# Paired steps of four gated networks: where the first weight sum is formed, and which buffer holds the second one's low part

## The chip, the cores and the metric

The kernel runs on one core of a Trainium2 chip. The metric is the device time of one execution in microseconds (us), as the median of several runs. TensorE multiplies matrices, VectorE (DVE), ScalarE (ACT) and GpSimd (POOL) work element by element, SyncE (SP) issues the loads. Each engine takes its own instructions in order, and they are tied together by semaphores.

## What is computed

A model of two blocks over 256 tokens of 1024 numbers each: several mixers, a routed mixture of experts, and four gated networks. The change touches the gated networks alone:

```python
def swiglu(x, w_gate, w_up, w_down):
    return (jax.nn.silu(x @ w_gate) * (x @ w_up)) @ w_down

f = swiglu(rms_norm_2(x, g[4]), ffn_w_gate[layer, 1], ffn_w_up[layer, 1], ffn_w_down[layer, 1])
x = x + 0.5 * rms_norm_2(f, g[5])
```

The hidden width is 2816. All weights are 32-bit.

## The kernel before

**Steps.** Each network (`ffn0` to `ffn3`) runs in 11 steps of 256 hidden columns. A step has three units of weights of 128x2048 numbers, 1 MB each: two for gate and up (the upper and the lower half of the 1024 inputs), one for down. A unit is loaded into a ring of five buffers (`ring`, `load`, L815 ff.), and then split for precision: ScalarE writes its high part (L994), VectorE its low part (L1718), both into one of four slots (`w_a`, `w_b`). TensorE multiplies high by high, high by low and low by high, three matmuls in place of one.

**Pairs.** Steps 3 and 4 are done together, and so are 7 and 8 (`PAIRS`). Tokens are halved, inputs are halved, and the two steps' columns are the halves of the output: a 2x2 by 2x2 product of blocks, done by the Winograd form of Strassen's scheme with seven products instead of eight. It needs four sums of the tokens' blocks (once a network) and four of the weights' blocks. With the units named b11 and b21 (step s) and b12 and b22 (step s+1), VectorE forms:

- t1 = b12 - b11, into the buffer `w_sum`
- t3 = b22 - b12, over b12 in the ring
- t2 = t3 + b11, over b11 in the ring
- t4 = b21 - t2, over b21 in the ring

t2, t4 and t1 are split too. Their high part goes, one after the other, into one buffer, `sum_hi` (ScalarE: L1401, L1411, L1416). The low part of t2 and t4 goes to `ring_lo`, a second buffer beside each buffer of the ring, that of t1 to `w_sum_lo` (VectorE, all by `sum_left`, L2385). t3 is split like any unit.

**TensorE's order in a pair** (`pair`, from L3487 on, `product` at L3479 with the lines L3483 to L3485, 12 matmuls each): the product of b11; the transpositions of step s-1 (L3440); m6 with t2; the product of b21; m7 with t3; half of step s-1's down product (L3449 to L3451); m4 with t4; the other half; the product of b22; the transpositions of step s; m5 with t1; step s's down product. The step before a pair is an ordinary one: gate and up (L3424 to L3426) in two halves, transpositions, down.

**VectorE's order around a pair** is written out by hand, in `gated` and `pair` (L2398 ff.). In step s-1: a product (`hid_made`, L2336), a low part of the turned one (`hid_left`, L2343), `weight_sums` (t1 at L2371, t3 at L2373), the split of b21, `hid_made`, `more_weight_sums` (t2 at L2378, t4 at L2380), t2's low part, two splits. Before the first pair of a network it also has `x_left` (L2392). In the pair: `hid_left`, c_12 (`joined`, L2395, after m6), the split of b22, `hid_made`, t4's low part, c_22 (after m7), the split of the next unit, c_21 (after m4), t1's low part, `hid_made`, and so on. ScalarE's order (`pair_ahead`, `pair`) mirrors it.

**The ring.** A buffer is loaded anew once its unit is split. The two buffers that hold t2 and t4 are freed by others (`RELEASE`): b11's by the end of m6 and b21's by the end of m4. The loads are in one queue, so each waits for those before it; the unit that goes to b11's buffer is the down unit of step s, the first that the pair still needs.

Of the kernel before, what the change touches and what calls it, by code (L numbers as in the profile page):

```python
# [9 lines left out]
ALU = mybir.AluOpType  # L10
# [13 lines left out]
RING = 5  # L24
# [246 lines left out]
def build(nc, x, gains, stream, small_1, cmp_w1, small_2, consts, slots, out):  # L271
# [3 lines left out]
    with ExitStack() as ctx:  # L275
# [14 lines left out]
        ring = sb("ring", [P, RING, UNIT])  # L290
# [377 lines left out]
        m_1, c_12, c_22, c_21 = (sm1[:, 512 * n:512 * n + 512] for n in range(4))  # L668

        FFNS = ["ffn0", "ffn1", "ffn2", "ffn3"]  # L670
        PAIR_DVE = ["t1", "t3", "t2", "t4", "t2_lo", "u2", "t4_lo", "u3", "c21", "t1_lo", "w", "c12", "c22"]
        FFN_DVE = ["x_raw", "s1", "s2", "s3", "s4", "s_lo"] + [f"{step}_{i}" for i in range(len(PAIRS)) for step in PAIR_DVE]
        FFN_ACT = ["s_hi"] + [f"{step}_{i}" for i in range(len(PAIRS)) for step in ("t2_hi", "m1", "t4_hi", "t1_hi")]
        FFN_PE = [f"{step}_{i}" for i in range(len(PAIRS)) for step in ("m6", "m7", "m4", "m5")]
# [1 line left out]
        def ffn_at(steps, name, step):  # L676

            return SPARSE_STEPS + FFNS.index(name) * len(steps) + steps.index(step) + 1
# [61 lines left out]
        for name in FFNS:  # L740
            for i, s in enumerate(PAIRS):
                b11, b21, _, _ = pair_units(name, s)
                RELEASE[b11] = ("ffn_pe", ffn_at(FFN_PE, name, f"m6_{i}"))
                RELEASE[b21] = ("ffn_pe", ffn_at(FFN_PE, name, f"m4_{i}"))

        def tops_done(name, s):
# [210 lines left out]
        def _(act):  # L957
# [414 lines left out]
            def gated(name):  # L1372
# [30 lines left out]
                def pair(i, s):  # L1403
                    b11, b21, _, _ = pair_units(name, s)
                    act.wait_ge(S("unit_used"), b11 + 1)
                    act.activation(m_1, bank[4][:, :], ACT.Copy).then_inc(S("ffn_act"), 1)
                    hid_in(s - 1, range(0, 2))
                    split_at(3 * s + 3)
                    act.wait_ge(S("ffn_dve"), ffn_at(FFN_DVE, name, f"t4_{i}"))
                    act.wait_ge(S("ffn_pe"), ffn_at(FFN_PE, name, f"m6_{i}"))  # L1410
                    act.activation(sum_hi[:, :], ring[:, b21 % RING, :], ACT.Copy).then_inc(S("ffn_act"), 1)  # L1411
                    act.wait_ge(S("unit_used"), b21 + 1)
                    silu_of(bank[4], 0)
                    split_at(3 * s + 4)
                    act.wait_ge(S("ffn_pe"), ffn_at(FFN_PE, name, f"m4_{i}"))
                    act.activation(sum_hi[:, :], w_sum, ACT.Copy).then_inc(S("ffn_act"), 1)  # L1416
                    act.wait_ge(S("ffn_dve"), ffn_at(FFN_DVE, name, f"c21_{i}"))
                    silu_of(c_21, 1)
                    split_at(3 * s + 5)
                    hid_in(s, range(0, 2))  # L1420
                    split_at(3 * s + 6)
                    for t, c in enumerate((c_12, c_22)):
                        act.wait_ge(S("ffn_dve"), ffn_at(FFN_DVE, name, f"c{t + 1}2_{i}"))
                        silu_of(c, t)
                    split_at(3 * s + 7)
                    split_at(3 * s + 8)
# [278 lines left out]
        def _(dve):  # L1705
# [619 lines left out]
            def gated(name):  # L2325
# [35 lines left out]
                    own("s2")  # L2361
                    dve.tensor_tensor(x_sum[:, 3], a12, x_sum[:, 1], ALU.subtract).then_inc(S("ffn_dve"), 1)

                def weight_sums(i, s):
                    b11, b21, b12, b22 = pair_units(name, s)
                    raw = [ring[:, b % RING, :] for b in (b11, b21, b12, b22)]
                    if i:
                        dve.wait_ge(S("ffn_pe"), ffn_at(FFN_PE, name, f"m5_{i - 1}"))
                    dve.wait_ge(S(f"unit{b11 % RING}"), 16 * (b11 // RING + 1))
                    dve.wait_ge(S(f"unit{b12 % RING}"), 16 * (b12 // RING + 1))  # L2370
                    dve.tensor_tensor(w_sum, raw[2], raw[0], ALU.subtract).then_inc(S("ffn_dve"), 1)  # L2371
                    dve.wait_ge(S(f"unit{b22 % RING}"), 16 * (b22 // RING + 1))
                    dve.tensor_tensor(raw[2], raw[3], raw[2], ALU.subtract).then_inc(S("ffn_dve"), 1)  # L2373

                def more_weight_sums(i, s):
                    b11, b21, b12, _ = pair_units(name, s)
                    own(f"t3_{i}")
                    dve.tensor_tensor(ring[:, b11 % RING, :], ring[:, b12 % RING, :], ring[:, b11 % RING, :], ALU.add).then_inc(S("ffn_dve"), 1)  # L2378
                    own(f"t2_{i}")
                    dve.tensor_tensor(ring[:, b21 % RING, :], ring[:, b21 % RING, :], ring[:, b11 % RING, :], ALU.subtract)\  # L2380
                       .then_inc(S("ffn_dve"), 1)
# [15 lines left out]
                def pair(i, s):  # L2397
                    b11, b21, _, b22 = pair_units(name, s)  # L2398
                    hid_left(s - 1, range(0, 2))
                    dve.wait_ge(S("ffn_act"), ffn_at(FFN_ACT, name, f"m1_{i}"))  # L2400
                    dve.wait_ge(S("ffn_pe"), ffn_at(FFN_PE, name, f"m6_{i}"))
                    joined(c_12, bank[7], m_1)
                    split_at(3 * s + 3)
                    hid_made(s, 0)
                    ring_left(f"t4_hi_{i}", b21)
                    dve.wait_ge(S("ffn_pe"), ffn_at(FFN_PE, name, f"m7_{i}"))
                    joined(c_22, bank[7], m_1)
                    split_at(3 * s + 4)
                    dve.wait_ge(S("ffn_pe"), ffn_at(FFN_PE, name, f"m4_{i}"))
                    joined(c_21, bank[7], m_1)  # L2410
                    sum_left(f"t1_hi_{i}", w_sum_lo, w_sum)
                    hid_made(s, 1, c_21)
                    dve.wait_ge(S("unit_used"), b22 + 1)
                    own(f"u2_{i}")
                    joined(c_12, bank[4], c_12)
                    hid_left(s, range(0, 2))
                    split_at(3 * s + 5)
                    dve.wait_ge(S("ffn_pe"), ffn_at(FFN_PE, name, f"m5_{i}"))
                    own(f"w_{i}")
                    joined(c_12, bank[5], c_12)  # L2420
                    joined(c_22, bank[5], c_22)
                    hid_made(s + 1, 0, c_12)
                    split_at(3 * s + 6)
                    hid_made(s + 1, 1, c_22)
                    split_at(3 * s + 7)
                    split_at(3 * s + 8)
# [6 lines left out]
                for s in range(1, last):  # L2433
# [7 lines left out]
                    if s + 2 == PAIRS[0]:  # L2441
                        x_whole()
                    if ahead is not None:
                        weight_sums(ahead, s + 1)
                    split_at(3 * s + 3)
                    hid_made(s, 1)
                    if ahead is not None:
                        more_weight_sums(ahead, s + 1)
                        ring_left(f"t2_hi_{ahead}", pair_units(name, s + 1)[0])
                    split_at(3 * s + 4)  # L2450
                    if s + 2 == PAIRS[0]:
                        x_sums()
# [397 lines left out]
        def _(pe):  # L2850
# [533 lines left out]
            def gated(name, then):  # L3384
# [103 lines left out]
                def pair(i, s):  # L3488
# [7 lines left out]
                    product(4, own[0], whole[0], True).then_inc(S("unit_used"), 1)  # L3496
                    turn(s - 1, range(0, 2))
                    sum_ready(f"t2_lo_{i}")
                    product(7, both[1], (sum_hi[:, :], ring_lo[:, b11 % RING, :]), True).then_inc(S("ffn_pe"), 1)
                    pe.wait_ge(S("ffn_act"), ffn_at(FFN_ACT, name, f"m1_{i}"))  # L3500
                    lo_ready(b21)
                    product(4, own[1], whole[1], False).then_inc(S("unit_used"), 1)
# [541 lines left out]
```

## Time and profile before

| | |
|---|---|
| runs, us | 1793.16, 1794.06, 1794.82 (median 1794.06) |
| profiled execution, us | 1793.34 |
| its span, us | 1790.4 |
| TensorE busy, us | 1754.3 (98%) |
| VectorE busy, us | 1389.7 (78%) |
| ScalarE busy, us | 995.0 (56%) |
| t1, L2371 | 8 times, 2280 ns in the median |

The profile is of one execution. The span runs from its first to its last instruction on the core; the execution's time is 2.9 us longer. A busy time is a sum over the whole span and doesn't say which wait ends last at a place, so the timelines of single stretches are needed. In them a row has a start, a duration and the engine, then line, operation and tensors. Brackets tell how long the engine was idle before and what released it. Starts of matmuls in a row are closer together than they are long, because they are pipelined.

### The profile page before, as it was taken

The numbers are of one execution on the slowest core, as the hardware profiler recorded it, in microseconds if no ns is written. First come the engines' busy times: TensorE is split into PE (matmuls) and PEld (weight loads), VectorE is DVE, ScalarE is ACT, GpSimd is POOL, SyncE is SP. The second block draws the span as 40 slices with busy tenths as digits, with TensorE's granted clock in tenths as the row PEclk, the third lists the DMA queues.
The fourth block names the chain that finished last, engine by engine and source line by source line (L and its number), as shares of the span: only waits on it lengthen the run. The fifth ranks groups of instructions, "written<-read, shape, count | busy, mean of one in ns | idle before, by whom it ended". The sixth has DMA issues, their size and how long they took to land.

```text
span 1790.4 us, 25225 instructions
## 1 busy us (share of the span) xinstructions
PE 1754.3 (98%) x10314; PEld 1482.6 (83%) x10314; DVE 1389.7 (78%) x1646; ACT 995.0 (56%) x1206; POOL 58.1 (3%) x98
## 2 busy tenths in 40 slices
PE   9999999999999999999999999999999999999998
PEld 8998898888888887787898988778877878787877
DVE  5349877788898898978498779886897667879784
ACT  5446653577777676645452355555555456656453
POOL 0040000000000001000000000000100010010000
PEclk9999999999999999999999999999999999999999
DMA  9343344699899897373442016527443745234631
GB/s 383 118 165 136 119 148 149 240 359 351 337 351 354 334 372 293 123 280 139 190 152 108 27 53 230 225 83 312 180 170 136 305 143 187 72 141 150 273 147 76
DMA packets 51379, 363.01 MB, mean 203 GB/s; under 512 B 5697, under 2 KB 5825, under 8 KB 8642
## 3 DMA queue, kind: packets, MB, share of 16 engines
q1 hardware_dynamic: 50976, 359.24, 52.6%
q8 instruction: 82, 1.34, 0.3%
q10 hardware_dynamic: 290, 2.17, 0.3%
q14 instruction: 31, 0.25, 0.0%
HBM read 360.34 MB, written 1.05 MB: 202 GB/s over the span
## 4 chain that ended last, share of the span: by engine, by line
PE 79%; DVE 15%; ACT 3%; issue 1%; DMA 1%; POOL 0%; DVEq 0%; POOLq 0%; ACTq 0%
PE bank L2866 8%; PE bank L3424 4%; PE bank L3426 4%; PE bank L3425 4%; PE bank L3451 3%; PE bank L3449 3%; PE bank L3450 3%; PE bank L3278 3%; PE bank L3280 3%; PE bank L3279 3%; DVE w_a L1718 3%; PE bank L3483 3%; PE bank L2924 3%; PE bank L3484 2%; PE bank L3485 2%; PE bank L3295 2%
## 5 line engine op out<-in xcount | busy, mean ns | idle before, releaser
L1718 DVE TENSOR_TENSOR w_a<-ring,w_a 128x2048 fp32r<-128x2048 f32 x220 | 500.4, 2287 | 132.5 <-ACT w_a L994 131.8
L994 ACT ACTIVATE w_a<-ring 128x2048 fp32r<-128x2048 f32 x219 | 416.2, 1913 | 121.4 <-PE bank L3451 42.1
L1718 DVE TENSOR_TENSOR w_b<-ring,w_b 128x2048 fp32r<-128x2048 f32 x63 | 144.1, 2287 | 29.3 <-ACT w_b L994 29.2
L994 ACT ACTIVATE w_b<-ring 128x2048 fp32r<-128x2048 f32 x63 | 120.5, 1912 | 36.2 <-PE bank L3426 17.8
L2866 PE MATMUL bank<-h,w_a 128*128 128x256 f32 x1040 | 137.3, 285 | 1.0 <-DVE ring_lo L1823 1.0
L2866 PEld LDWEIGHTS bank<-h,w_a 128*128 128x128 f32 x1040 | 128.8, 191 | 4.1 <-issue 3.0
L3449 PE MATMUL bank<-w_a,hid 128*128 128x512 f32 x280 | 109.9, 393 | 0.0
L3451 PE MATMUL bank<-w_a,hid 128*128 128x512 f32 x280 | 109.2, 390 | 0.0
L3450 PE MATMUL bank<-w_a,hid 128*128 128x512 f32 x280 | 109.0, 389 | 0.0
L3424 PE MATMUL bank<-w_a,h 128*128 128x512 f32 x240 | 95.0, 396 | 0.5 <-DVE w_a L1718 0.5
L3426 PE MATMUL bank<-w_a,h 128*128 128x512 f32 x240 | 93.7, 390 | 0.0
L3425 PE MATMUL bank<-w_a,h 128*128 128x512 f32 x240 | 93.4, 389 | 0.0
L1391 ACT ACTIVATE sil<-bank,tiny 128x256 f32<-128x256 f32 x64 | 30.4, 474 | 101.0 <-PE bank L3426 98.9
L3278 PE MATMUL bank<-w_a,xg 128*128 128x512 f32 x192 | 77.1, 402 | 0.0
L3280 PE MATMUL bank<-w_a,xg 128*128 128x512 f32 x192 | 75.0, 391 | 0.0
L3279 PE MATMUL bank<-w_a,xg 128*128 128x512 f32 x192 | 74.8, 390 | 0.0
L978 ACT ACTIVATE arena<-bank 128x512 f32<-128x512 f32 (+2 forms) x47 | 26.8, 571 | 74.8 <-PE bank L2866 54.8
L881 POOL TENSOR_SCALAR tiny<-tiny 128x1 f32<-128x1 f32 x20 | 10.7, 533 | 1588.7 <-ACT junk L1012 1002.4
L3451 PEld LDWEIGHTS bank<-w_a,hid 128*128 128x128 f32 x280 | 52.6, 188 | 11.2
L2336 DVE SCALAR_TENSOR_TENSOR hid<-bank,tiny,sil 128x256 f32<-128x256 f32 x64 | 30.7, 480 | 39.9 <-ACT sil L1391 39.9
L3450 PEld LDWEIGHTS bank<-w_a,hid 128*128 128x128 f32 x280 | 52.6, 188 | 10.9
L3449 PEld LDWEIGHTS bank<-w_a,hid 128*128 128x128 f32 x280 | 52.6, 188 | 10.8
(648 smaller groups left out, 4201.1 us busy)
## 6 DMA issues: line engine op xcount, KB each, us to landing
ring<-in_stream SPq DMA_DIRECT2D x330, 1024.0 KB, 5.3
G<-in_gains SPq DMA_DIRECT2D x14, 512.0 KB, 7.8
cmp_area<-in_cmp_w ACTq DMA_DIRECT2D x1, 2048.0 KB, 11.3
sm<-in_small SPq DMA_DIRECT2D x1, 1582.0 KB, 12.0
con<-in_consts SPq DMA_DIRECT2D x1, 1032.0 KB, 15.9
X<-in_x SPq DMA_DIRECT2D x2, 512.0 KB, 4.0
out_x<-X SPq DMA_DIRECT2D x4, 256.0 KB, 2.0
sm<-in_small SPq DMA_DIRECT2D x1, 730.5 KB, 22.5
```

The lines of the kernel that those rows point to most:

```text
L994: act.activation(w_slot(unit)[:, 0, :], ring[:, unit % RING, :], ACT.Copy).then_inc(S("w_hi"), 1)
L1718: dve.tensor_tensor(w_slot(unit)[:, 1, :], ring[:, unit % RING, :], w_slot(unit)[:, 0, :].bitcast(FP32), ALU.subtract).then_inc(S("w_lo"), 1)
L2866: ins = pe.matmul(ps, w(wp, k), xp[:, k, :], start=(a == 0 and k == 0), stop=(a == 2 and k == terms - 1))
L3278: pe.matmul(bank[4][:, :], x_hi, w[0][:, k, :], start=(half == 0 and k == 0), stop=False)
L3279: pe.matmul(bank[4][:, :], x_hi, w[1][:, k, :], start=False, stop=False)
L3280: ins = pe.matmul(bank[4][:, :], x_lo, w[0][:, k, :], start=False, stop=(half == 1 and k == 3))
L3424: pe.matmul(bank[4 + t][:, :], x_hi, w[0][:, k, :], start=first, stop=False)
L3425: pe.matmul(bank[4 + t][:, :], x_hi, w[1][:, k, :], start=False, stop=False)
L3426: ins = pe.matmul(bank[4 + t][:, :], x_lo, w[0][:, k, :], start=False, stop=end)
L3449: pe.matmul(ps, x_hi, w[0][:, f, d], start=(s == 0 and f == 0), stop=False)
L3450: pe.matmul(ps, x_hi, w[1][:, f, d], start=False, stop=False)
L3451: return pe.matmul(ps, x_lo, w[0][:, f, d], start=False, stop=(s == last and f == 1))
```

## The change

- t1 is no longer formed ahead of the pair but inside it, on VectorE after c_12 (`first_sum`), and as b22 - t2. This is the same sum, because t2 = b22 - b12 + b11. b11's buffer has held t2 since then, and b22 is still as it was loaded.
- `weight_sums` becomes `third_sum`, with t3 alone; the wait for b11's load moves to t2.
- t2's low part goes to `w_sum_lo` instead of `ring_lo`; t1's low part takes that buffer later, as before.
- b11's buffer is freed by t1 instead of m6, since t1 reads t2 there.
- ScalarE waits for t1 before it makes its high part.

```diff
-        PAIR_DVE = ["t1", "t3", "t2", "t4", "t2_lo", "u2", "t4_lo", "u3", "c21", "t1_lo", "w", "c12", "c22"]
+        PAIR_DVE = ["t3", "t2", "t4", "t2_lo", "u2", "t1", "t4_lo", "u3", "c21", "t1_lo", "w", "c12", "c22"]
...
-                RELEASE[b11] = ("ffn_pe", ffn_at(FFN_PE, name, f"m6_{i}"))
+                RELEASE[b11] = ("ffn_dve", ffn_at(FFN_DVE, name, f"t1_{i}"))
...
+                    act.wait_ge(S("ffn_dve"), ffn_at(FFN_DVE, name, f"t1_{i}"))
                     act.wait_ge(S("ffn_pe"), ffn_at(FFN_PE, name, f"m4_{i}"))
                     act.activation(sum_hi[:, :], w_sum, ACT.Copy).then_inc(S("ffn_act"), 1)
...
-                def weight_sums(i, s):
-                    b11, b21, b12, b22 = pair_units(name, s)
-                    raw = [ring[:, b % RING, :] for b in (b11, b21, b12, b22)]
-                    if i:
-                        dve.wait_ge(S("ffn_pe"), ffn_at(FFN_PE, name, f"m5_{i - 1}"))
-                    dve.wait_ge(S(f"unit{b11 % RING}"), 16 * (b11 // RING + 1))
-                    dve.wait_ge(S(f"unit{b12 % RING}"), 16 * (b12 // RING + 1))
-                    dve.tensor_tensor(w_sum, raw[2], raw[0], ALU.subtract).then_inc(S("ffn_dve"), 1)
-                    dve.wait_ge(S(f"unit{b22 % RING}"), 16 * (b22 // RING + 1))
-                    dve.tensor_tensor(raw[2], raw[3], raw[2], ALU.subtract).then_inc(S("ffn_dve"), 1)
+                def third_sum(i, s):
+                    _, _, b12, b22 = pair_units(name, s)
+                    for b in (b12, b22):
+                        dve.wait_ge(S(f"unit{b % RING}"), 16 * (b // RING + 1))
+                    dve.tensor_tensor(ring[:, b12 % RING, :], ring[:, b22 % RING, :], ring[:, b12 % RING, :], ALU.subtract)\
+                       .then_inc(S("ffn_dve"), 1)
+
+                def first_sum(i, s):
+                    b11, _, _, b22 = pair_units(name, s)
+                    dve.tensor_tensor(w_sum, ring[:, b22 % RING, :], ring[:, b11 % RING, :], ALU.subtract).then_inc(S("ffn_dve"), 1)
...
                     joined(c_12, bank[7], m_1)
+                    first_sum(i, s)
                     split_at(3 * s + 3)
...
                     if ahead is not None:
-                        weight_sums(ahead, s + 1)
+                        third_sum(ahead, s + 1)
                     split_at(3 * s + 3)
                     hid_made(s, 1)
                     if ahead is not None:
                         more_weight_sums(ahead, s + 1)
-                        ring_left(f"t2_hi_{ahead}", pair_units(name, s + 1)[0])
+                        sum_left(f"t2_hi_{ahead}", w_sum_lo, ring[:, pair_units(name, s + 1)[0] % RING, :])
...
-                    product(7, both[1], (sum_hi[:, :], ring_lo[:, b11 % RING, :]), True).then_inc(S("ffn_pe"), 1)
+                    product(7, both[1], (sum_hi[:, :], w_sum_lo), True).then_inc(S("ffn_pe"), 1)
```

## Rows read from the trace of the kernel before

**Rows 1.** The page: busy time of each engine, and the granted clock in 40 slices.

```profile
PE 1754.3 (98%) x10314; PEld 1482.6 (83%) x10314; DVE 1389.7 (78%) x1646; ACT 995.0 (56%) x1206; POOL 58.1 (3%) x98
PEclk9999999999999999999999999999999999999999
```

**Rows 2.** Waits (us, times, longest); durations of L2385 (min/median/max ns).

```profile
PE bank L3483 <- DVE ring_lo L2385: 9.6, 8, 1.4
...
L2385 DVE TENSOR_TENSOR y<-F,sum_hi x8: 2291/2293/2295, 772.4 to 1732.8; 128x2048 fp32r<-128x2048 f32 x8
```

**Rows 3.** Timeline of VectorE, second pair of the first network.

```profile
808.64 2.28 DVE L2371 TENSOR_TENSOR F<-ring 128x2048 f32<-128x2048 f32 x1
810.84 2.28 DVE L2373 TENSOR_TENSOR ring<-ring 128x2048 f32<-128x2048 f32 x1
813.04 2.28 DVE L1718 TENSOR_TENSOR w_a<-ring,w_a 128x2048 fp32r<-128x2048 f32 x1
...
820.16 2.28 DVE L2385 TENSOR_TENSOR ring_lo<-ring,sum_hi 128x2048 fp32r<-128x2048 f32 x1
...
827.37 0.68 DVE L2395 TENSOR_TENSOR sm<-bank,sm 128x512 f32<-128x512 f32 x1
...
830.56 2.28 DVE L2385 TENSOR_TENSOR ring_lo<-ring,sum_hi 128x2048 fp32r<-128x2048 f32 x1
```

**Rows 4.** Timeline of ScalarE, same stretch.

```profile
810.21 1.92 ACT L994 ACTIVATE w_a<-ring 128x2048 fp32r<-128x2048 f32 x1 [2.21 <-PE bank L3426]
...
830.55 1.92 ACT L994 ACTIVATE w_a<-ring 128x2048 fp32r<-128x2048 f32 x1 [1.75 <-DMA ring<-in_stream]
```

**Rows 5.** Timeline of TensorE, same stretch.

```profile
820.83 0.60 PE L3440 MATMUL bank<-con,hid 128*128 128x128 f32 x4
822.50 0.50 PE L3483 MATMUL bank<-sum_hi,xs_hi 128*128 128x512 f32 x1 [1.06 <-DVE ring_lo L2385]
...
825.38 0.39 PE L3483 MATMUL bank<-w_a,h 128*128 128x512 f32 x1
...
822.50 0.19 PEld L3483 LDWEIGHTS bank<-sum_hi,xs_hi 128*128 128x128 f32 x1 [1.30 <-DVE ring_lo L2385]
...
833.71 0.39 PE L3483 MATMUL bank<-sum_hi,h 128*128 128x512 f32 x1
...
836.49 0.40 PE L3449 MATMUL bank<-w_b,hid 128*128 128x512 f32 x1
...
842.05 0.60 PE L3440 MATMUL bank<-con,hid 128*128 128x128 f32 x4
842.41 0.48 PE L3483 MATMUL bank<-sum_hi,xs_hi 128*128 128x512 f32 x1
```

**Rows 6.** Loads: issues (start, us); then loads issued from 799, from 836.6, to landing.

```profile
800.71 0.33 SPq L821 DMA_DIRECT2D ring<-in_stream  x1
...
825.57 11.44 SPq L821 DMA_DIRECT2D ring<-in_stream  x2
...
ring<-in_stream SPq DMA_DIRECT2D x1, 1024.0 KB, 5.6
...
ring<-in_stream SPq DMA_DIRECT2D x5, 1024.0 KB, 9.0
```

**Rows 7.** Timelines, first pair of the first network: VectorE, ScalarE, TensorE.

```profile
746.78 2.28 DVE L1718 TENSOR_TENSOR w_a<-ring,w_a 128x2048 fp32r<-128x2048 f32 x1
...
764.29 2.29 DVE L2385 TENSOR_TENSOR ring_lo<-ring,sum_hi 128x2048 fp32r<-128x2048 f32 x1
...
743.65 1.92 ACT L994 ACTIVATE w_a<-ring 128x2048 fp32r<-128x2048 f32 x1 [2.21 <-PE bank L3426]
...
767.46 0.40 PE L3483 MATMUL bank<-sum_hi,h 128*128 128x512 f32 x1
```

**Rows 8.** Timelines, first pair of the third network: VectorE, ScalarE.

```profile
1301.92 2.28 DVE L1718 TENSOR_TENSOR w_a<-ring,w_a 128x2048 fp32r<-128x2048 f32 x1
...
1299.08 1.92 ACT L994 ACTIVATE w_a<-ring 128x2048 fp32r<-128x2048 f32 x1 [2.49 <-PE bank L3426]
```

More of the change, by code:

```diff
@@ L2377, in more_weight_sums @@
                     own(f"t3_{i}")
+                    dve.wait_ge(S(f"unit{b11 % RING}"), 16 * (b11 // RING + 1))
                     dve.tensor_tensor(ring[:, b11 % RING, :], ring[:, b12 % RING, :], ring[:, b11 % RING, :], ALU.add).then_inc(S("ffn_dve"), 1)
```

## The prediction

> **What bounds the kernel now.** I read the page first: TensorE is busy for 1754.3 of 1790.4 us, at its full clock (2.4 GHz, granted 1.0), so only its idle time and what delays it count [rows 1]. Next the list of waits: in the lines of the paired products, TensorE waits 8 times, once a pair, for the low part that VectorE forms at L2385 [rows 2]. That total leaves out part of the idle time, because the ends of matmuls are modelled; the wait's price comes from the timeline.
>
> Then one pair, the second of the first network, engine by engine. VectorE works without a gap from 808.64 to 832.84: t1, t3, a split, a product of step s-1, t2, t4, t2's low part, two splits, two short ones, the split of b22, a short one, t4's low part [rows 3]. ScalarE has the high halves ready before VectorE wants them, the first at 810.21 + 1.92 = 812.13, and it waits for TensorE before that one [rows 4]. TensorE ends four transpositions that begin at 820.83 and starts the first product of sums (m6) only at 822.50. Where nothing holds it, a product follows such a group 0.36 us after its start (842.05 to 842.41), so it could have started at 821.19: it stands 1.31 us [rows 5].
>
> The second place to watch is the product of m4, at 833.71. It reads t4's low part, which ends at 830.56 + 2.28 = 832.84, and TensorE doesn't wait: the cover is 0.87 us, or 0.81 us with the 0.06 us that m6 starts after its own operand's end (820.16 + 2.28 = 822.44 to 822.50) [rows 3, 5].
>
> **What goes: t1 ahead of the pair.** It took 2.28 us, 2.20 from its start to the next [rows 3]. t3 then starts at 808.64 and ends at 810.92. Its operand b22, the last of the loads, was issued at 800.71 and took 5.6 us, so it is there at 806.3 [rows 6]. But the split behind t3 needs ScalarE's half of 812.13, which TensorE's progress sets and the change doesn't move; a split starts 0.03 to 0.04 us behind it. So it starts at 812.17 where it was 813.04: the gain is 0.87 us, not 2.20, and VectorE idles 1.33 us where it had none. All that follows is unbroken, so t2's low part ends at 821.57 and m6 starts at 821.63: 0.87 us earlier, with 0.44 us of waiting left.
>
> In the first pair of a network VectorE is later, because of x_left: the split starts at 746.78, ScalarE's half ends at 745.57, so the gain is 1.17 us [rows 7]. In the third network ScalarE's half ends at 1301.00, against a split at 1301.92, and the gain is 0.88 us [rows 8].
>
> **What comes: t1 inside the pair.** It stands in VectorE's queue between the join of c_12 and the split of b22, so ahead of that split, of hid_made, of t4's low part and of the join of c_22. Same form, same size: 2.20 us more ahead of t4's low part. That now ends at 832.84 - 0.87 + 2.20 = 834.17, and m4's product can start at 834.23 instead of 833.71. TensorE would have come there at 832.84, so it stands 1.39 us in a place where it stood for nothing: the gain at m6 is all spent, and 0.52 us more. A product of 12 matmuls behind a wait took 2.88 us (822.50 to 825.38) against 2.78 us for the one that didn't wait (833.71 to 836.49) [rows 5]; the new wait adds this 0.10. So a second pair loses 0.62 us.
>
> First pairs: t4's low part ends at 764.29 + 2.29 - 1.17 + 2.20 = 767.61, the product starts at 767.67 instead of 767.46, and with the 0.10 the loss is 0.31 us [rows 7]. In the third network's first pair the gain is 0.29 us smaller than in the other first pairs, so the loss is 0.60 us [rows 8]. The other pairs repeat these two patterns to 0.03 us.
>
> **The 0.10 is the disputed small term.** The row: m6's first weight load starts at 822.50, with its matmul and not before, though TensorE had been idle [rows 5]. The Trainium skill (TensorE: Matmul & The Clock Gate, "Step-by-step: what each phase is for") says that TensorE's queue pulls weight loads ahead of matmuls in flight; were this load pulled ahead of the wait, the new wait would cost 8 x 0.10 = 0.8 us less. The row speaks against it: the load waits for the same thing.
>
> **The moved release.** The slot of b11 is freed by t1's end instead of m6's. t1 runs from 827.10 (the join of c_12, 827.37, less 0.87, plus 0.60) to 829.38, so the load behind it is issued at 829.41 instead of 825.57. Before, ScalarE waited for it until 830.55, 5.0 us behind the issue [rows 4, 6]; so it is there at 834.4. ScalarE splits it 834.4 to 836.3, VectorE 836.3 to 838.6. Behind them are queued: on VectorE the join of c_21 (838.5 to 839.2), t1's low part and hid_made; on ScalarE t1's high part, which has to wait for m4 anyway (837.3 to 839.2). So t1's low part runs 839.3 to 841.6 and hid_made ends at 842.0. TensorE asks for that at 834.23 + 2.88 + 5.56 = 842.67 (836.49 to 842.05, the two blocks between [rows 5]). The cover is 0.7 us, the cost nothing; from a landing over 5.8 us it costs as much as it is late. The load behind it waits for m4 (its issue ended at 837.01, 0.5 us behind m4's product [rows 5, 6]), and shifts with TensorE, as do all that follow. The new wait on ScalarE for t1 is met 7 us before it is reached. Nothing is queued differently on GpSimd; the gain rows' loads wait for the pair's last product and shift with it.
>
> **Small things.** t2's low part goes to the other buffer: 2.293 us there in the median [rows 2], against 2.28 [rows 3]: 0.01 us a pair. Blocks differ a little in pace: m4's took 2.78 us, the two behind it 5.56 us [rows 5]. I take no change of it.
>
> **The sum.** 3 x 0.31 + 0.60 + 4 x 0.62 = 4.0 us slower. TensorE is back to back between pairs, so each loss reaches the end. The profiled execution took 1793.34 us (span 1790.4), 0.72 us below the median of the runs: 1797.3 for such an execution, 1798.1 for the median.
>
> **Rivals.**
> (a) VectorE's new idle time doesn't arise, because ScalarE's half is ready when t3 ends. Then t2's low part comes 2.20 us earlier and m6's whole wait goes; t4's low part keeps its place, m4's product starts at 832.90, 0.81 us earlier, and 0.10 is paid: 0.71 us won a pair, 5.7 in all, 1788.4. It decides at ScalarE's end, 812.13 against 810.92. Against it: ScalarE's idle time before that half is ended by TensorE, in first and second pairs alike [rows 4, 7].
> (b) The change does not do what it says ahead of the pair: t3 waits for b22 as late as t1's old end, and nothing is won at m6. Then m4's product is 2.20 - 0.81 = 1.39 us late, with 0.10 1.5 us a pair, 12 us in all: 1806. It decides at a landing after 808.64; the row has 806.3.
> (c) The late load costs. The five loads issued from 836.68 on, which share the DMA engines, take 9.0 us in the median. Were the late one to take 2 us more than its 5.0, hid_made would end 1.2 us behind TensorE's arrival, and with 0.10 every pair would pay 1.3 us, 10 us on top of the 4: 1808. It decides at 5.8 us. Against it: at 829.4 nothing else is in flight, and the next load is issued about 836.7, after its landing [rows 6].
> (d) The weight load is pulled ahead in the new wait: 3.2 us, 1797.3.
>
> **How the numbers follow.** Forecast, with net losses of 3.5 to 5.5 us or a little less: 0.74; (a) 0.07; (b) 0.03; (c) 0.06; (d) 0.10. A measurement of this kernel tells about 0.2%, 3.6 us, from no change. The forecast's 4.0 is just beyond that, and the runs of before are 0.8 us either way of their median; so of its 0.74 I put 0.47 beyond and 0.27 within; (d) is mostly within. Slower 0.57, same 0.36, faster 0.07. Range: down to 3.2 less the 0.8 of the runs and a little of unseen cover, 1796.0; up to 4.5 plus 0.8 and a part of (c), in some pairs only, 1801.0.
>
> **What would show it.** In the profile of after: m6's wait about 0.4 us in each pair; a new wait of 1.4 us at m4's product, released by L2385's line; VectorE idle about 1.3 us before the split behind t3, released by ScalarE; ScalarE's wait for the ring's DMA longer by 3.9 us; no wait at the second transpositions. The forecast is wrong if m4's product isn't held, if m6's wait stays over 1 us, or if a wait for hid_made appears.

## The result, and the profile after

The kernel after the change takes 1807.63 us in the median of six runs (1802.45 to 1813.66), the kernel before 1793.38 us (1791.3 to 1794.82). The ratio is 1.0082, with a 95% interval of 1.006 to 1.0104: slower by 14.3 us, where 4.0 were forecast, and outside of the range. The profiled execution of after took 1802.45 us, 9.1 more than that of before, so the profile shows the smaller part of it. A second set of four runs of the same kernel, further down, gave 1806.0 us.

One thing that was said of the buffers ahead of the prediction is to be set right: `ring_lo` is no second buffer beside the ring. It is the same memory, and a low part is written over its raw weights, as t1's is written over t1 (`w_sum`, shown as F, and `w_sum_lo`, shown as y, are one buffer). So the kernel before frees b11 only at m6's end, and the kernel after puts t2's low part into t1's buffer so that t2 stays readable there.

The page of after:

```profile
span 1800.1 us, 25241 instructions
...
PE 1755.6 (98%) x10314; PEld 1480.7 (82%) x10314; DVE 1390.0 (77%) x1646; ACT 994.9 (55%) x1206; POOL 58.2 (3%) x98
```

The instructions are the same in number and in busy time as in [rows 1]. The waits of after (us in all, times, longest):

```profile
ACT w_a L994 <- DMA ring<-in_stream: 62.1, 18, 6.5
...
PE bank L3486 <- DVE sm L2397: 14.5, 8, 1.8
```

[rows 2] had 9.6 us of TensorE's waits in the paired products, released by the low part. After has 14.5 us, again once a pair, but the releaser is another one: `sm<-bank,sm`, L2397. That is not a low part. It is a join, the addition of a bank of PSUM to a short sum. It stands ahead of m4's product. TensorE in the second pair of the first network:

```profile
821.70 0.60 PE L3443 MATMUL bank<-con,hid 128*128 128x128 f32 x4
822.49 0.50 PE L3486 MATMUL bank<-sum_hi,xs_hi 128*128 128x512 f32 x1 [0.19 <-DVE y L2387]
...
835.68 0.50 PE L3486 MATMUL bank<-sum_hi,h 128*128 128x512 f32 x1 [1.83 <-DVE sm L2397]
```

Here the first line is the transpositions, the second m6, the third m4's product. This pair begins 0.87 us later than before's (821.70 against 820.83 [rows 5]), because the first pair has lost that much; that it is also the gain at m6 is chance. I count from there. m6 starts 0.79 us behind the transpositions' start, before 1.67 [rows 5]. m4's product starts 13.98 us behind it, before 12.88 [rows 5] (13.99 and 12.87 before rounding, the figures used further down). VectorE in the same pair:

```profile
809.48 2.28 DVE L2369 TENSOR_TENSOR ring<-ring 128x2048 f32<-128x2048 f32 x1
813.02 2.29 DVE L1719 TENSOR_TENSOR w_a<-ring,w_a 128x2048 fp32r<-128x2048 f32 x1 [1.26 <-ACT w_a L994]
...
820.15 2.28 DVE L2387 TENSOR_TENSOR y<-ring,sum_hi 128x2048 fp32r<-128x2048 f32 x1
...
827.36 0.68 DVE L2397 TENSOR_TENSOR sm<-bank,sm 128x512 f32<-128x512 f32 x1
827.96 2.28 DVE L2374 TENSOR_TENSOR F<-ring 128x2048 f32<-128x2048 f32 x1
830.15 2.28 DVE L1719 TENSOR_TENSOR w_a<-ring,w_a 128x2048 fp32r<-128x2048 f32 x1
832.75 2.28 DVE L2387 TENSOR_TENSOR ring_lo<-ring,sum_hi 128x2048 fp32r<-128x2048 f32 x1
834.95 0.68 DVE L2397 TENSOR_TENSOR sm<-bank,sm 128x512 f32<-128x512 f32 x1
```

t3 is now first, the split behind it waits 1.26 us for ScalarE, and t1 (F) stands behind the join of c_12. t4's low part ends at 832.75 + 2.28 = 835.03. The product doesn't start then. It starts at 835.68, 0.05 us behind the end of the next line, the join of c_22 (834.95 + 0.68 = 835.63). That join reads bank 7, which m4's product then adds to, so it has to be done first; the code says so with `sum_ready(f"u3_{i}")` ahead of m4's product. In the kernel before the same join is this row of VectorE's timeline:

```profile
832.76 0.68 DVE L2395 TENSOR_TENSOR sm<-bank,sm 128x512 f32<-128x512 f32 x1
```

It ended at 833.44, and the product started at 833.71 [rows 5]. The cover was 0.27 us, or 0.21 with the 0.06 from an operand's end to a start. The prediction has 0.81.

### The profile page after: what moved, and what is told of

The parts are those of the page before. It is cut to its first block, busy times and chain, and to the rows that moved or that the text cites. A ratio compares the mean times of both kernels' runs of the same rounds, so it can differ in the third digit from the quotient of the medians.

```text
span 1800.1 us, 25241 instructions
## 1 busy us (share of the span) xinstructions
PE 1755.6 (98%) x10314; PEld 1480.7 (82%) x10314; DVE 1390.0 (77%) x1646; ACT 994.9 (55%) x1206; POOL 58.2 (3%) x98
## 4 chain that ended last, share of the span: by engine, by line
PE 76%; DVE 17%; ACT 3%; issue 2%; DMA 1%; POOL 0%; DVEq 0%; POOLq 0%; ACTq 0%
PE bank L2869 8%; PE bank L3427 4%; PE bank L3429 4%; PE bank L3428 4%; DVE w_a L1719 4%; PE bank L3281 3%; PE bank L3283 3%; PE bank L3282 3%; PE bank L3454 3%; PE bank L3452 3%; PE bank L3453 3%; PE bank L2927 3%; PE bank L3298 2%; PE bank L3300 2%; PE bank L3299 2%
```

## The experiments

**Theories for the first batch.** *Join*: m4's product waits for the join of c_22, so all that is put ahead of this join costs; 0.60 us a pair more than forecast. *Low part*: it waits for t4's low part, as the prediction has it, and the rest comes from elsewhere. *Load*: the later release of b11 costs (rival (c)). Four kernels: t1 taken away, the release alone, t1 between the low part and the join, t1 behind the join.

**no_t1** is after with t1 left out; t1's two splits and m5 use other data, so that m5's part of the output is not computed. b11's slot is then freed by the join of c_12, so the later release is gone as well.

```diff
-                    act.wait_ge(S("ffn_dve"), ffn_at(FFN_DVE, name, f"t1_{i}"))
                     act.wait_ge(S("ffn_pe"), ffn_at(FFN_PE, name, f"m4_{i}"))
-                    act.activation(sum_hi[:, :], w_sum, ACT.Copy).then_inc(S("ffn_act"), 1)
+                    act.activation(sum_hi[:, :], f_hi[:, :, :].rearrange("p t n -> p (t n)").bitcast(FP32), ACT.Copy).then_inc(S("ffn_act"), 1)
...
                     joined(c_12, bank[7], m_1)
-                    first_sum(i, s)
```

> The changed kernel without t1: no first sum at all, b11's buffer is freed by the join of c_12, and m5 multiplies split data of another sum (so what m5 adds is not the reference's). Join theory: in the changed kernel m4's product was held by the join of c_22 (its third wait), which stands behind t1 and t4's low part; with t1 gone from there nothing is held, m6 keeps its gain of 0.8 us (second pairs) and 1.1 us (first pairs): 7.7 us faster than before, about 1785.5, and the granted clock has no stretches beyond those of before. Low-part theory (the step of the prediction): the same time. A rival, that the late release of b11 or the other buffer for the low part costs of itself: no faster than before.

Measured: 1783.5 us, ratio to before 0.9943 (0.9927 to 0.996); span 1781.4 us. No wait is left at m4's product, and m6 comes 1.17 or 0.87 us earlier, as it does in after. So the gain at m6 is real and as large as forecast, and what costs is t1 at its new place or the later release that goes with it; the next three kernels separate the two.

**rel_only** is before with one edit: b11's slot is freed later, by b22's split.

```diff
-                RELEASE[b11] = ("ffn_pe", ffn_at(FFN_PE, name, f"m6_{i}"))
+                RELEASE[b11] = LO[b22]
```

> The kernel before with one change: b11's buffer is freed when b22's low part is written (830.3 us in the second pair of the first network) instead of by m6 (825.5), which is just when the changed kernel frees it. Join theory and prediction: the load lands near 835.2, the second transpositions aren't held, within 0.2% of before (1793.4). Rival (the late load costs): 4 us and more slower.

Measured: 1798.03 us in the median of ten runs, ratio 1.0027 (1.0018 to 1.0037). It was expected to cost nothing, and that was a miss. What L3440, the second transpositions, waited for (us, times), between 700 and 1790 us:

```profile
its engine sat idle before it (us, times) until:
  DVE hid L2336: 11.8, 16
```

In before this line has no such entry. Matmuls and their weight loads both count here; by the starts of matmuls it is 0.4 to 0.7 us in each of seven pairs. In the last pair TensorE waited longest:

```profile
1743.23 0.66 PE L3440 MATMUL bank<-con,hid 128*128 128x128 f32 x4 [1.58 <-DVE hid L2336]
```

The load was issued at 1729.73 and took 5.99 us there, against 4.7 to 5.0 in the other pairs. So a late release does reach TensorE: rival (c)'s mechanism is real, and here it costs even where the load takes its usual time. In after it costs nothing in seven pairs: t1 ends some 1 us earlier in the pair than b22's split does here, and TensorE is itself held at m4's product. In the eighth the load took 6.42 us, and the weight load of the second transpositions waited:

```profile
1744.85 0.42 PEld L3443 LDWEIGHTS bank<-con,hid 128*128 128x128 f32 x4 [0.37 <-DVE hid L2337]
```

The transpositions then began 0.1 us later than in the other pairs.

**t1_between** is after with t1 behind t4's low part and ahead of the join of c_22. Its load comes later, so the down unit's split is moved behind `hid_made`, where it holds nothing; the two parts of step s's transposed product (`hid_in`, `hid_left`) are moved up to stand right behind that split.

```diff
-                    first_sum(i, s)
                     split_at(3 * s + 3)
                     hid_made(s, 0)
                     ring_left(f"t4_hi_{i}", b21)
+                    first_sum(i, s)
...
                     joined(c_22, bank[7], m_1)
-                    split_at(3 * s + 4)
...
                     hid_made(s, 1, c_21)
+                    split_at(3 * s + 4)
+                    hid_left(s, range(0, 2))
```

> The changed kernel with t1 behind t4's low part and still ahead of the join of c_22; the split of step s's down unit moved behind hid_made, so that the later load holds nothing. Join theory: m4's product starts as late as in the changed kernel (near 14.0 us after the start of the transpositions, with a wait of 1.8 us), so the time is that of the changed kernel, 1801 to 1808. Low-part theory: t4's low part is ready 2.2 us earlier, m4's product isn't held, and the time is near 1786.

Measured: 1806.29 us, ratio 1.0074 (1.0057 to 1.0091). VectorE and TensorE around m4's product, in the same pair:

```profile
831.17 2.29 DVE L2387 TENSOR_TENSOR ring_lo<-ring,sum_hi 128x2048 fp32r<-128x2048 f32 x1
833.37 2.29 DVE L2374 TENSOR_TENSOR F<-ring 128x2048 f32<-128x2048 f32 x1
835.57 0.69 DVE L2397 TENSOR_TENSOR sm<-bank,sm 128x512 f32<-128x512 f32 x1
...
836.31 0.50 PE L3486 MATMUL bank<-sum_hi,h 128*128 128x512 f32 x1 [1.81 <-DVE sm L2397]
```

t4's low part is done at 833.46, and TensorE stands idle for 1.81 us more, until the join is done at 836.26. That decides between *join* and *low part*: the low part is early and nothing is won. The moved split doesn't cost or win either, since the time is that of after.

**t1_late_split** has t1 one place further, behind that join, and the down unit's split moved as in t1_between.

```diff
                     joined(c_22, bank[7], m_1)
-                    split_at(3 * s + 4)
+                    first_sum(i, s)
```

> As t1_between, but t1 behind the join of c_22. Join theory: m4's product isn't held, m6 keeps its gain, t1's buffer is freed near 834.8 us of the second pair, the down unit's low part is there just as its product is due (0 to 0.2 us of waiting): 1786 to 1788, 5 to 8 us faster than before. Low-part theory: the same as t1_between. Were the late load to cost, there would be a wait of over 0.5 us at step s's down product in each pair and the time would be 1791 or more.

Measured: 1786.87 us, ratio 0.9959 (0.9945 to 0.9973). TensorE doesn't wait at m4's product any more; what held L3486's lines is this (us, times):

```profile
its engine sat idle before it (us, times) until:
  DVE y L2387: 5.6, 16
  DVE sm L2397: 1.7, 8
```

The 5.6 are what is left of m6's wait, counted once for matmuls and once for weight loads. The 1.7 aren't m4's: they are the first weight loads of m7's product, which wait 0.2 us a pair for the join of c_12, as in before (1.8 us, 8 times). After has 34.1 us in the line of the join instead of 1.7, with matmuls and weight loads both counted. One instruction of 2.2 us, moved by 0.68 us of other work, changes the time by 19.4 us (1806.29 to 1786.87).

**What the first batch left open.** With the join, the loss comes to 8.8 us (the 4.0 forecast and 8 x 0.60 more), not to the 14.3 of the medians. Runs of after differ by 11 us, and the longer a run, the lower its mean granted clock: 1802.45 us at 0.998, 1807.24 at 0.995, 1813.66 at 0.992. In the profile of after one stretch stands out, behind the wait of the seventh pair:

```profile
1667.32 0.50 PE L3486 MATMUL bank<-sum_hi,h 128*128 128x512 f32 x1 [1.83 <-DVE sm L2397]
1667.65 0.40 PE L3487 MATMUL bank<-ring_lo,h 128*128 128x512 f32 x1
1667.89 0.52 PE L3488 MATMUL bank<-sum_hi,h 128*128 128x512 f32 x1
1668.21 0.63 PE L3486 MATMUL bank<-sum_hi,h 128*128 128x512 f32 x1
1668.63 0.63 PE L3487 MATMUL bank<-ring_lo,h 128*128 128x512 f32 x1
```

The matmuls begin 0.23 us apart, then 0.43. The next block starts 4.45 us behind m4's start; in the other seven pairs it is 2.89. *Clock*: behind the new wait the clock falls to its lower level in some pairs of some runs, about 1.56 us each time. *Clock by chance*: such stretches are spread over the kernel and have nothing to do with the wait. Four kernels: after once more, to see another of its executions; half of t1 at the old place, for a shorter wait; the same without a wait at m4; and a longer wait at another place.

**after_again** is after, unchanged.

> The changed kernel once more, for the spread of its time. Clock theory: beyond 8 times 1.1 us of waits it has stretches at half clock behind m4's wait, in some pairs and not in others, each costing 1.6 us; so its runs spread over 1801 to 1814 and the slower a run, the lower its mean granted clock. Rival: the spread belongs to the chip, and the kernel before spreads as much on it.

Measured: 1806.0 us (four runs, 1802.62 to 1809.69), ratio 1.0074 (1.0054 to 1.0093). The kernel before, in 14 runs beside it, went from 1790.07 to 1793.83 us, a spread of 3.8 against 7.1, so the spread isn't the chip's alone. The profiled execution is the longest of the four, 1809.69 us. Its m4 product in the second pair:

```profile
838.26 0.50 PE L3486 MATMUL bank<-sum_hi,h 128*128 128x512 f32 x1 [1.83 <-DVE sm L2397]
838.59 0.40 PE L3487 MATMUL bank<-ring_lo,h 128*128 128x512 f32 x1
838.83 0.54 PE L3488 MATMUL bank<-sum_hi,h 128*128 128x512 f32 x1
839.17 0.63 PE L3486 MATMUL bank<-sum_hi,h 128*128 128x512 f32 x1
```

The same stretch as a window (its ends, length, the busy time of PE, PEld, DVE, ACT and POOL with instructions, then the granted clock, the share of the DMA engines and GB/s):

```profile
838.20:842.00 3.80, 3.74 (x10) 2.98 (x11) 2.29 (x2) 1.27 (x1) 0.00 (x0) 0.59 0.00 0
```

The granted clock is 0.59. Five of the eight pairs have such a stretch (m4's products at 769, 838, 1145, 1214 and 1675 us), each right behind the wait, and m5 comes 1.5 to 1.6 us later in them than in the other three. TensorE's end is 16.1 us behind before's: 8.9 that the eight pairs lose in any case (worked out further down) and 5 x 1.56 = 7.8, less 0.6 in small differences.

**t1_half** forms the first half of t1 ahead of the pair and the second half inside it. The low part of t2 is made in two halves, in the two places that are free by then.

```diff
+                    dve.tensor_tensor(w_sum[:, 0:UNIT // 2], ring[:, b12 % RING, 0:UNIT // 2], ring[:, b11 % RING, 0:UNIT // 2], ALU.subtract)\
+                       .then_inc(S("ffn_dve"), 1)
...
-                    dve.tensor_tensor(w_sum, ring[:, b22 % RING, :], ring[:, b11 % RING, :], ALU.subtract).then_inc(S("ffn_dve"), 1)
+                    dve.tensor_tensor(w_sum[:, UNIT // 2:], ring[:, b22 % RING, UNIT // 2:], ring[:, b11 % RING, UNIT // 2:], ALU.subtract)\
+                       .then_inc(S("ffn_dve"), 1)
```

> The changed kernel with half of t1's columns formed ahead of the pair, as b12 - b11, in the time that VectorE idles there, and the other half inside at the changed kernel's place; t2's low part is written as two halves in two buffers for that. In the pair VectorE has 1.1 us more than before instead of 2.2. Join theory: m6 keeps its gain but for 0.07 us, m4's product waits 0.9 instead of 1.8 us and starts 0.1 us later than before in second pairs, 0.2 earlier in first ones: within 2 us of before (1792.4), and no stretch at half clock behind it. Low-part theory: m4's product waits 0.3 us, and the time is 4 us under before, 1788.

Measured: 1793.92 us (ten runs), ratio 1.0015 (1.0006 to 1.0025). The wait at m4's product is 0.75 us, that at m6 0.27 in second pairs and 0.47 to 0.54 in first ones, and no stretch at the lower clock follows.

```profile
834.15 0.50 PE L3497 MATMUL bank<-sum_hi,h 128*128 128x512 f32 x1 [0.75 <-DVE sm L2401]
```

**t1_half_late** has the second half behind the join of c_22 instead, with the down unit's split moved.

> As t1_half, with the inner half behind the join of c_22 and the split of the down unit moved behind hid_made. Join theory: nothing is held but m6 by 0.25 us, the late load lands 1 us sooner than in t1_late_split, so step s's down product isn't held either: 7.5 us faster than before, 1785, 1 to 2 us under t1_late_split. If the extra instruction of the low part and its wait cost more than 0.1 us a pair: 1787.

Measured: 1785.65 us, ratio 0.9963 (0.9949 to 0.9978). With nothing in front of the join, the half makes no difference that can be told from t1_late_split; the 1 to 2 us that were expected over it are not there.

**pad_ahead** is before with t1 formed twice at its old place.

```diff
+                    link(dve.tensor_tensor(w_sum, raw[2], raw[0], ALU.subtract))
                     dve.tensor_tensor(w_sum, raw[2], raw[0], ALU.subtract).then_inc(S("ffn_dve"), 1)
```

> The kernel before with t1 formed twice ahead of each pair (the first result is overwritten by the same): 2.3 us more on VectorE, all of it in m6's wait, which becomes 3.6 to 3.9 us. Without an effect on the clock: 8 times 2.3, 18 us slower, 1811. Clock theory: waits this long are followed by half-clock stretches in most pairs, up to 8 times 1.6 us more, 1817 to 1824, and the mean granted clock is 0.990 to 0.993 instead of 0.998. Rival (the half-clock stretches of the changed kernel come from m4's place, where the wait is the second in one pair): 1811 at 0.998.

Measured: 1824.82 us, ratio 1.018 (1.0163 to 1.0197). The wait at m6 is now 3.37 to 3.70 us, and what follows runs at the lower clock from its second matmul on:

```profile
830.25 0.79 PE L3484 MATMUL bank<-sum_hi,xs_hi 128*128 128x512 f32 x1 [3.40 <-DVE ring_lo L2386]
830.84 0.63 PE L3485 MATMUL bank<-ring_lo,xs_hi 128*128 128x512 f32 x1
831.27 0.63 PE L3486 MATMUL bank<-sum_hi,f_hi 128*128 128x512 f32 x1
```

Two windows, around this wait and around that of the fifth pair:

```profile
829.00:833.00 4.00, 2.75 (x7) 2.17 (x8) 4.00 (x3) 4.00 (x5) 0.00 (x0) 0.61 0.00 0
1325.00:1335.00 10.00, 6.30 (x30) 4.98 (x29) 9.96 (x7) 9.48 (x7) 0.00 (x0) 1.00 0.06 13
```

The granted clock is 0.61 and 1.00. Seven of the eight pairs have such a stretch; the fifth hasn't, with a wait of the same length. TensorE's last matmul starts 31.6 us later than in before. The longer waits are 8 x 2.33 = 18.6 of it; of the other 13.0 the seven pairs take 12.5, 1.8 us each in the mean. Pair by pair it is 1.3 to 1.5 us in five of them, and 2.6 and 2.7 in the two where the stretch is twice as long. So the lower clock belongs to the wait and not to the change, and behind a longer wait it came in more pairs.

**The last batch** asked whether the late load alone can hold the pair, and whether the 1.26 us that VectorE idles in after can be put to use.

**t1_late** has t1 behind the join of c_22 and nothing else moved.

```diff
-                    first_sum(i, s)
...
                     joined(c_22, bank[7], m_1)
+                    first_sum(i, s)
```

> The changed kernel with t1 behind the join of c_22 and nothing else moved: the split of the down unit stays ahead of t1's high part on ScalarE. Its load is freed 9 us later than before. From the rows of t1_late_split (load landed 18.7 us after the transpositions' start): split to 20.7, t1's high part to 22.5, low part to 24.9, hid_made to 25.3, against TensorE's arrival at 20.3: a new wait of 4.9 us at the second transpositions of every pair, 39 us, less the 7.7 won at m6, and up to 13 us of half-clock stretches: 1823 without them, 1830 to 1837 with them. Rival (the moved release is harmless wherever it is, as the prediction had it): 1786.

Measured: 1849.73 us, ratio 1.0316 (1.0298 to 1.0335); more than was expected. The timelines of VectorE and TensorE:

```profile
840.28 2.28 DVE L2374 TENSOR_TENSOR F<-ring 128x2048 f32<-128x2048 f32 x1
849.36 2.29 DVE L1719 TENSOR_TENSOR w_a<-ring,w_a 128x2048 fp32r<-128x2048 f32 x1 [6.80 <-ACT w_a L994]
851.57 0.68 DVE L2397 TENSOR_TENSOR sm<-bank,sm 128x512 f32<-128x512 f32 x1
852.17 2.28 DVE L2387 TENSOR_TENSOR y<-F,sum_hi 128x2048 fp32r<-128x2048 f32 x1
854.37 0.48 DVE L2337 SCALAR_TENSOR_TENSOR hid<-sm,tiny,sil 128x256 f32<-128x256 f32 x1
...
854.90 1.11 PE L3443 MATMUL bank<-con,hid 128*128 128x128 f32 x4 [5.78 <-DVE hid L2337]
```

t1 frees the slot at 842.56; the load behind it is split only from 849.36 on, and in VectorE's queue the join of c_21, t1's low part and `hid_made` stand behind that split. TensorE waits 5.8 us. The expectation had left the join of c_21 out of that row of work, which is 0.6 us. All eight pairs have the lower clock behind this wait: TensorE's last matmul starts 56.9 us later than in before, of which the waits are 46.8 less the 7.8 won at m6, and the other 17.9 are 2.2 a pair. Rival (c), then, is a matter of how late: where the change puts t1, some 5.4 us earlier in the pair, TensorE has no such wait in seven pairs of eight.

**t2_first** is after with t2 formed right behind t3, ahead of the split that waits for ScalarE.

```diff
                         third_sum(ahead, s + 1)
+                        second_sum(ahead, s + 1)
                     split_at(3 * s + 3)
                     hid_made(s, 1)
                     if ahead is not None:
-                        more_weight_sums(ahead, s + 1)
+                        fourth_sum(ahead, s + 1)
```

> The changed kernel with t2 formed right behind t3, ahead of b21's split, in the 1.3 us in which VectorE waits there for ScalarE. Everything on VectorE up to the join of c_22 comes 1.3 us sooner. Idle-time theory (the loss is VectorE's idle time plus the join's small cover): m6 isn't held at all, m4's product waits 1.1 us and starts 0.2 us earlier than in the kernel before; with the 0.1 behind a wait and 0.1 for waits between neighbouring sums: 1791 to 1793, the same as before, with no half-clock stretches. Rival (t1's place inside the pair costs 2 us whatever stands ahead of it): 1800 or more.

Measured: 1791.25 us (ten runs), ratio 0.9993 (0.9984 to 1.0003). m6's wait is gone, and the wait at m4's product is 0.97 us in second and 1.28 in first pairs, none of it followed by the lower clock. With t1 where the change puts it, the kernel is level with before.

**t2_first_late** is t2_first with t1 behind the join of c_22 and the down unit's split moved, as in t1_late_split.

> t2_first and t1_late_split together. m6's wait of 1.3 us (second pairs) and 1.6 us (first pairs) goes whole, m4's product isn't held, the late load is freed 0.9 us earlier against TensorE than in t1_late_split: 8 times 1.45, 11.6 us less than before, 1780.5; 1783 if a wait between the sums or at the down product eats 0.3 us a pair.

Measured: 1780.85 us (1779.7 to 1781.43), ratio 0.9931 (0.9917 to 0.9944): 12.3 us faster than before and the best of all. VectorE has no idle time between t3 and the split now, and TensorE doesn't stand anywhere in the pair. VectorE's timeline, then two windows of 50 us over the first network's two pairs (PE's busy time is the first number behind the length):

```profile
807.91 2.28 DVE L2369 TENSOR_TENSOR ring<-ring 128x2048 f32<-128x2048 f32 x1
810.23 2.29 DVE L2380 TENSOR_TENSOR ring<-ring 128x2048 f32<-128x2048 f32 x1
812.43 2.29 DVE L1719 TENSOR_TENSOR w_a<-ring,w_a 128x2048 fp32r<-128x2048 f32 x1
```

```profile
740.00:790.00 50.00, 50.00 (x228) 41.06 (x227) 45.36 (x33) 28.24 (x24) 0.00 (x0) 1.00 0.41 161
800.00:850.00 50.00, 50.00 (x226) 41.08 (x225) 42.03 (x31) 28.76 (x23) 0.00 (x0) 1.00 0.41 161
```

Its gain is m6's whole idle time: 1.61 us in first and 1.31 in second pairs, 11.7 us in all; the eight pairs of its trace gain 11.8.

## Why the prediction was wrong

**Right, to a few hundredths.** Counted from the start of the pair's transpositions:
- The split behind t3 was forecast for 812.17, 8.66 us ahead of it; it came 8.68 ahead (813.02 against 821.70), held by ScalarE. Rival (a) did not occur.
- m6 was forecast to start 0.80 us behind it and came at 0.79. In one first pair it is 1.07, as forecast, but in the second network's instead of the third's; where ScalarE is 0.28 us late changes from trace to trace (in no_t1 it is the third network's again). The profile gives m6's remaining wait as 0.19 us, counted from the modelled end of the transpositions; counted from 0.36 us behind their start, where an unheld product begins, it is 0.43, where 0.44 was forecast.
- t4's low part was forecast to end at 834.17, 13.34 behind it. It ended at 835.03, 13.33.
- The block behind the new wait takes 2.89 us instead of 2.78: the 0.10 is there, and rival (d) is out. Of weight loads pulled ahead, which the Trainium skill tells of (TensorE: Matmul & The Clock Gate, "Step-by-step: what each phase is for"), neither wait shows any: both blocks pay.
- The load behind b11 was expected 13.6 us behind the transpositions' start; ScalarE starts its split, which ended a wait for the DMA, at 835.16, 13.5 behind. There is no wait at the second transpositions in seven pairs. In the last the load took 6.42 us, beyond the prediction's 5.8, and cost 0.1 us; that it wasn't 0.6 is luck, because TensorE came 0.60 us later than forecast. Rival (b) did not occur either: t3 starts at once.

**The failed step: the cover at m4's product.** The prediction says that this product reads t4's low part and that "the cover is 0.87 us, or 0.81 us". It does read that, but the last thing it waits for is the join of c_22, one instruction further on. With that row the same working gives 833.44 - 0.87 + 2.20 + 0.06 = 834.83, against 833.71: 1.12 us late instead of 0.52. Measured: 13.99 against 12.87 behind the transpositions, 1.12. In a first pair 0.81 instead of 0.21, measured 0.77 to 0.82 in three of the four, and 1.08 in the one where ScalarE is late (1.10 by this working). So every pair loses 0.60 us more: 4.0 + 8 x 0.60 = 8.8 us. The pairs of after's trace, summed in this way, lose 8.0 at m4's product and 0.9 in the block behind it, 8.9. t1_between and t1_late_split, which differ by the side of the join on which t1 stands, show it: 1806.29 and 1786.87 us. In the list of waits of before nothing points to the join of c_22, since TensorE didn't wait there at all. The same list does have an entry for the sister case, which the prediction passed over: m7's product waits for the join of c_12, once a pair.

```profile
PEld bank L3483 <- DVE sm L2395: 1.8, 8, 0.2
```

**The missing term: the clock behind the new wait.** It wasn't in the sum, nor among the rivals. The prediction took the clock of before as granted in full, where the execution has 0.998, and the trace of before itself holds the case: a wait of 1.79 us outside of the pairs, with the lower clock right behind it (0.43 us from one matmul to the next, here 1449.41 to 1449.84).

```profile
1447.42 1.69 PE L2881 MATMUL bank<-con,F 128*128 128x128 f32 x8 [1.79 <-DVE F L1759]
...
1449.41 0.63 PE L3876 MATMUL bank<-w_a,h 128*128 128x512 f32 x1
1449.84 0.63 PE L3875 MATMUL bank<-w_a,h 128*128 128x512 f32 x1
```

After has the same wait at the same place without the lower clock; the difference there is 1.3 us. Behind the new wait a stretch at the lower clock costs 1.56 us, and after's profiled execution has one: 8.9 + 1.6 - 1.3 = 9.2 us, where TensorE's end moved by 8.7; the remaining 0.5 is spread over small differences in pace. The median run lies 14.3 - 8.9 = 5.4 us above that, which is three to four stretches in eight pairs. That those runs have them is inferred from their clock (0.993 and 0.995 for the two around the median) and from after_again, which at 0.995 shows five; they weren't profiled themselves.

**The range** reached up by "a part of (c)". The mis-sized cover alone takes the time to 1798.1 + 4.8 = 1802.9, beyond its 1801.0. Rival (c)'s number, 1808, is near the measured one, but not by its mechanism: in after TensorE is held by `hid_made` at the second transpositions in the last pair alone, by 0.1 us, and in after_again nowhere. The prediction's threshold for it, though, took TensorE's lateness at m4's product into its 0.7 us of cover; rel_only, where TensorE isn't late and the load is issued 1 us later in the pair, has no cover at all.

**Why the change loses, in short.** What m6 gains is capped at 0.87 or 1.17 us by ScalarE; t1 costs 2.20 us wherever TensorE is close behind VectorE, and in front of the join of c_22 it is 0.2 us behind. Behind that join there is room for it, if the down unit's split makes way.

## What to carry to other kernels

Before something is put into a queue, find the last thing that each waiting instruction behind it needs, by its code and all of its semaphores, and read the cover off that row: an operand may be there while an accumulator's bank is still being read. Look also for what is queued behind that place, and move a step to where the consumer's last condition is already met; 0.68 us further on was worth 19 us here. A new wait on TensorE is priced with what the clock may do behind it, and several runs, not one profile, tell how often it does.

## What the hardware showed that was not expected

**TensorE's clock can fall behind a wait of 1.8 us.** In all these kernels TensorE is over 95% busy. Shorter waits in the pairs (up to 1.37 us in before, 1.28 in t2_first, 1.58 in rel_only) were followed by no lower clock in the profiled executions. Behind the 1.8 us at m4's product it came in one of eight pairs (after), in two (t1_between) and in five (after_again), at 1.56 us each. Behind 3.4 to 3.7 us in seven of eight (pad_ahead, 1.8 us each in the mean), behind 5.7 to 6.2 us in all eight (t1_late, 2.2 us each). The wait of 1.79 us outside of the pairs, which all 13 traces have, was followed by it in three (before, rel_only, pad_ahead). The matmuls are then 0.43 us apart instead of 0.23, the levels of 1.2 and 2.4 GHz. The Trainium skill (TensorE: Matmul & The Clock Gate, "What's actually happening") says that there are only these two, and that the count of matmuls at the lower one at the start of one kernel varies from run to run. These traces show only these two levels, and stretches at the lower one in the middle of a kernel that vary from run to run as well (one in after, five in after_again). The waits differ in what stands ahead of them as well (products or transpositions), and what of this decides, wait or place, no run here separates.

**A load of 1 MB that is alone takes 4.7 to 5.0 us in most pairs, but in some far longer:** 5.99 us in rel_only's last pair, 6.42 in after's last, 6.64 in t1_half's second, where the transpositions behind it began 0.3 us late. A cover below 1 us at a place where one load is waited for is not safe in every pair.
